# First norm of a hybrid decoder layer: root on ScalarE alone, whole-tile evictions on VectorE, another order of loads and signals

## The chip, the cores and the metric

One core of a Trainium2 chip runs the whole layer in one launch. The metric is the device time of one execution in microseconds (us), the median over runs. All data is float32.

## The reference, cut to what matters

One layer of a decoder trunk over 528 rows (16 learned meta tokens, then 512 tokens) of 1024 channels:

```
h = concat(meta_tokens, x)                       # 528 x 1024
n = h * rsqrt(mean(h*h, -1) + 1e-6) * norm1_g    # the first norm: what the change touches
u = n @ w_in                                     # 1024 x 6213 columns for three mixers and the gates
u_shift = u[:, :1280] + (previous row - u[:, :1280]) * rwkv_mu
y_a = RWKV-7 time mixing of u_shift   (6 heads of 64, chunks of 64 steps)
y_b = stick-breaking attention        (5 heads)
y_c = forgetting attention            (5 heads)
h = h + (sum_i sigmoid(G_i) * (y_i @ W_i)) @ w_out
h = h + MoE(rms_norm(h) * norm2_g)    # 16 experts, 2 of one group of 4 for each token
return h[16:]
```

## The kernel before

The kernel gives every engine one program, written out by hand, and orders them by counting semaphores. A helper `done` adds one to a semaphore and lets the same engine wait for it, so the instructions of ACT, DVE and POOL run strictly one after the other on their engine. No planner is at work. What one engine does next is the order of its block in the file.

**Loads (SP, L370 to L398).** SP asks for the meta rows, the four 128-row tiles of x (`h[:, t, :]`, 512 KB each), the norm's weights `g1` (1024 values that land as 128 x 8, one value at a time), three pieces of w_in (1 MB each, 256 columns, that is two chunks of 128), and then 21 small parameter transfers that all count on `params_in`. The fourth piece waits until the first has been used.

**First norm (L662 to L697 on ACT, L938 to L968 on DVE, L1384 to L1397 on PE).** For the meta rows, and then for each of the four tiles, ACT squares and sums a row (L675, L688; the sum comes out by a read of the accumulator, listed under the same line). DVE makes the mean and adds 1e-6 (L947, L959), ACT takes logarithm and exponential with factor -0.5 (L671, L672), DVE scales the rows (L949, L964), PE turns them by eight transposes into PSUM (L1387, L1395), and the eviction multiplies with `g1` and writes the turned rows `nT`. Of each tile DVE evicts chunks 0 to 3 in one instruction (L955) and ACT chunks 4 to 7 in four (L684). Ahead of tile 0's mean, DVE waits for `g1` (L950) in its program order. A constant `eps_c` (1e-6) is set on DVE after all of that (L968).

**Shifted columns (PE L1421 to L1447).** PE multiplies `nT` with ten chunks of 128 columns. One chunk has two halves of 264 rows, and 32 MATMUL records in the trace. Ahead of chunk n (from n = 2 on) it waits until chunk n-2 has been moved out of PSUM by ACT (L745), and ahead of both halves of chunk 0 it waits for the evictions of tiles 0 and 1, and 2 and 3. ACT's first eviction stands behind its wait for all 21 parameter transfers (L696, L697). DVE, behind the same wait, scales the router's weights (L970), clears padding (L975, L976) and mixes each chunk with its shifted copy (L982, L983). After chunk 1 is mixed ACT takes a tanh (L748) that the two low-rank products of chunks 2 to 4 need (L1400, L1406).

**Constants (POOL, L517 to L562).** POOL builds the masks one after another, with level masks for the later triangular inverses (L540 to L555), a row `reset` for the running sums, and some index rows. One signal at the end, `consts_ready`, counts 1 for all of them. DVE waits for it at L999, ahead of its first running sum (L987, which reads `reset`), PE at L1439 ahead of its first sum over heads (which reads `head_ones`). The level masks are first read by DVE at L1052.

After that PE works through projections for the attentions, the scan of the time mixing, both attentions, gate products, the output projection and the experts.

Of the kernel before, what the change touches and what calls it, by code (L numbers as in the profile page):

```python
# [14 lines left out]
ALU = mybir.AluOpType  # L15
# [3 lines left out]
P = 128  # L19
# [79 lines left out]
def hybrid_layer(nc, x, meta, g1, w_in, mu, w_up, w0, a_up, a0, k_k, k_a, r_k, ln_g, ln_b, f_b, q_g, k_g,  # L99
# [4 lines left out]
    with ExitStack() as ctx:  # L104
# [264 lines left out]
        def _(sp):  # L369
            sp.dma_start(metax[0:META, :], meta).then_inc(sem("meta_in"), 16)  # L370
            for t in range(NT):
                sp.dma_start(h[:, t, :], x[t * P:(t + 1) * P, :]).then_inc(sem(f"tile_in{t}"), 16)
            sp.dma_start(g1c, g1.rearrange("(c p) -> p c", p=P)).then_inc(sem("g1_in"), 16)
# [134 lines left out]
        def _(pool):  # L508
# [28 lines left out]

            for lv in range(6):
# [17 lines left out]
            done(g.memset(reset[:], 1.0))  # L556
            done(g.memset(reset[:, 0:L:CH], 0.0))
# [105 lines left out]
        def _(act):  # L663
# [6 lines left out]
            def inverse_root(z, s):  # L670
# [3 lines left out]
            act.wait_ge(sem("meta_in"), 16)  # L674
            done(a.activation(tmp_shift[0:META, :, :].rearrange("p a b -> p (a b)")[:, 0:D], metax[0:META, :], ACT.Square,  # L675
                              accum_out=stat[0:META, 4:5]), "ss_ready")
            act.wait_ge(sem("ms_ready"), 1)
            inverse_root(stat[0:META, 4:5], "rstd_ready")

            def high_chunks_out(t):  # L680
                act.wait_ge(sem("xT_psum"), t + 2)
                for c in range(T_SPLIT, DC):
                    o = 1024 * t + c * P
                    ins = a.activation(nT[:, c, META + t * P:META + (t + 1) * P], psf[:, o:o + P], ACT.Copy, scale=g1c[:, c:c + 1])  # L684
                done(ins, "nT_high")
# [253 lines left out]
        def _(dve):  # L939
# [3 lines left out]

            for j in range(SC):
                done(v.memset(U[:, j, 0:1], 0.0))
            dve.wait_ge(sem("ss_ready"), 1)
            done(ts(stat[0:META, 4:5], stat[0:META, 4:5], 1.0 / D, EPS, ALU.mult, ALU.add), "ms_ready")  # L947
            dve.wait_ge(sem("rstd_ready"), 1)
            done(ts(metax[0:META, :], metax[0:META, :], stat[0:META, 4:5], None, ALU.mult), "xs_ready")  # L949
            dve.wait_ge(sem("g1_in"), 16)  # L950
            gain = lambda c1, n: g1c[:, 0:c1].rearrange("p (c a) -> p c a", a=1).broadcast_to([P, c1, n])

            def low_chunks_out(t):
                dve.wait_ge(sem("xT_psum"), t + 2)
                done(tt(nT[:, 0:T_SPLIT, META + t * P:META + (t + 1) * P],  # L955
                        psf[:, 1024 * t:1024 * t + T_SPLIT * P].rearrange("p (c n) -> p c n", c=T_SPLIT), gain(T_SPLIT, P), ALU.mult), "nT_low")
# [985 lines left out]
```

## Time and profile before

| | us |
|---|---|
| median of 3 runs | 935.89 (935.33 to 936.1) |
| the profiled execution | 936.31 |
| its span in the trace | 934.6 |
| PE busy | 874.3 (94%) |
| DVE, ACT, POOL busy | 285.3, 196.8, 100.9 |
| mean granted TensorE clock | 0.974 of full |

PE is TensorE's matrix products, PEld its weight loads, DVE is VectorE, ACT is ScalarE, POOL is GpSimd, SPq the queue that issues transfers. Times in the rows are counted from the start of the span. "Releaser" is what ended an idle time. The granted clock is a share of 2.4 GHz, so 0.50 is 1.2 GHz. The profiled execution's time is 1.7 us more than its span, and 0.4 us more than the median.

### The profile page before, as it was taken

The page shows a single profiled execution, that of the slowest core. Times are in us where ns is not written, and L with a number is a line of the kernel's source. Part 1 is how long each engine was busy: PE and PEld are TensorE (multiplying, and loading weights), DVE is VectorE, ACT ScalarE, POOL GpSimd, SP SyncE. Part 2 cuts the span into 40 slices and gives each one's busy share as a digit, 9 for nine tenths or more (in the row PEclk, how much of TensorE's full clock was granted, in tenths as well). Part 3 has the DMA queues.
Part 4 walks back from the last instruction along what each step waited for, and adds up shares of the span by engine and source line. Part 5 has one row for each costly group of instructions (what it writes and reads, how often), then busy time and mean ns, then how long its engine had stood idle before and what let it go on. Part 6 is the DMA issues. An engine that isn't in the chain of part 4 may idle for free.

```text
span 934.6 us, 16279 instructions
## 1 busy us (share of the span) xinstructions
PE 874.3 (94%) x6948; PEld 505.8 (54%) x6948; DVE 285.3 (31%) x587; ACT 196.8 (21%) x390; POOL 100.9 (11%) x225
## 2 busy tenths in 40 slices
PE   3999999999998999999999999997999957999995
PEld 3878888877776765445454444443445542333331
DVE  3244811312312222452302244333531143222212
ACT  5135111122026111241412121143002220111100
POOL 7720000000003100011000000000000001212121
PEclk9999999999999999999999999998999967999998
DMA  8212136000000000047111112025565077899972
GB/s 228 58 46 88 47 80 193 2 2 3 2 3 1 3 3 25 23 101 199 46 50 32 50 54 68 1 76 177 168 230 227 22 282 281 290 380 386 384 274 110
DMA packets 76135, 109.76 MB, mean 117 GB/s; under 512 B 16891, under 2 KB 61067, under 8 KB 71968
## 3 DMA queue, kind: packets, MB, share of 16 engines
q1 hardware_dynamic: 71296, 93.22, 29.3%
q0 software_dynamic: 4768, 15.52, 5.7%
q8 instruction: 55, 0.90, 0.4%
q14 instruction: 16, 0.13, 0.0%
HBM read 100.32 MB, written 10.50 MB: 119 GB/s over the span
## 4 chain that ended last, share of the span: by engine, by line
PE 90%; DVE 3%; DMA 2%; ACT 2%; issue 1%; SPq 0%; DVEq 0%; POOL 0%; POOLq 0%; ACTq 0%
PE ps L1489 18%; PE ps L1514 10%; PE ps L1841 9%; PE ps L1466 8%; PE ps L1433 8%; PE ps L1793 6%; PE ps L1754 5%; PE ps L1867 5%; PE ps L1471 4%; PE ps L1828 1%; PE ps L1669 1%; PE ps L1737 1%; PE ps L1711 1%; DMA arena<-in_w_p_fox 1%; PE ps L1687 1%
## 5 line engine op out<-in xcount | busy, mean ns | idle before, releaser
L1489 PE MATMUL ps<-arena 128*128 128x512 f32 x304 | 142.9, 608 | 0.0
L1489 PEld LDWEIGHTS ps<-arena 128*128 128x128 f32 x304 | 54.8, 191 | 62.6 <-issue 60.7
L1841 PE MATMUL ps<-arena 128*32 128x512 f32 x624 | 86.0, 598 | 0.1
L1514 PEld LDWEIGHTS ps<-arena 64*64 64x64 f32 x2376 | 73.3, 134 | 23.7 <-issue 13.7
L1514 PE MATMUL ps<-arena 64*64 64x64 f32 x2376 | 80.3, 220 | 1.6 <-ACT arena L780 1.3
L1433 PE MATMUL ps<-arena 128*128 128x264 f32 x320 | 74.8, 393 | 0.6 <-PE ps L1433 0.6
L1433 PEld LDWEIGHTS ps<-arena 128*128 128x128 f32 x320 | 61.2, 193 | 13.5 <-issue 1.8
L1466 PE MATMUL ps<-arena,h 128*128 128x264 f32 x256 | 65.5, 397 | 0.5 <-PE ps L1433 0.5
L1754 PE MATMUL ps<-yT_all,arena 128*128 128x512 f32 x112 | 52.6, 623 | 5.3 <-DMA arena<-in_w_p_fox 5.1
L1793 PE MATMUL ps<-arena 128*128 128x512 f32 x128 | 56.2, 594 | 0.0
L1466 PEld LDWEIGHTS ps<-arena,h 128*128 128x128 f32 x256 | 45.9, 188 | 9.6 <-issue 0.8
L1841 PEld LDWEIGHTS ps<-arena 128*32 128x32 f32 x624 | 22.9, 109 | 45.1 <-issue 45.1
L1867 PE MATMUL ps<-arena 128*32 128x512 f32 x384 | 43.7, 594 | 0.6 <-DVE arena L1309 0.6
L1471 PE MATMUL ps<-arena 128*128 128x320 f32 (+1 forms) x128 | 42.7, 458 | 0.0
L1292 DVE TENSOR_TENSOR arena<-ps,chan 128x512 f32<-128x512 f32 x24 | 15.6, 686 | 83.4 <-PE ps L1828 83.3
L603 POOL DMA_INDIRECT arena<-n_rows,idx x12 | 11.8, 983 | 259.5 <-DVE idx L1276 252.7
L1754 PEld LDWEIGHTS ps<-yT_all,arena 128*128 128x128 f32 x112 | 21.6, 198 | 32.3 <-issue 25.4
L1793 PEld LDWEIGHTS ps<-arena 128*128 128x128 f32 x128 | 23.7, 189 | 28.2 <-issue 28.2
L1489 PE MATMUL ps<-arena,yT_all 128*128 128x512 f32 x80 | 38.1, 608 | 0.3 <-PE ps L1617 0.3
L1841 PE MATMUL ps<-yT_all,arena 128*32 128x512 f32 x144 | 36.4, 602 | 0.0
L780 ACT ACTIVATE arena<-ps 128x576 f32<-128x576 f32 x15 | 9.8, 652 | 81.7 <-PE ps L1514 81.7
L1042 DVE COPY arena<-ps 128x512 f32<-128x512 f32 x16 | 10.9, 680 | 50.0 <-PE ps L1489 50.0
(342 smaller groups left out, 1019.4 us busy)
## 6 DMA issues: line engine op xcount, KB each, us to landing
arena<-in_moe_w_down SPq DMA_DIRECT2D x32, 512.0 KB, 15.9
arena<-in_moe_w_gate SPq DMA_DIRECT2D x13, 1024.0 KB, 11.0
arena<-in_moe_w_up SPq DMA_DIRECT2D x13, 1024.0 KB, 16.3
arena<-in_w_in SPq DMA_DIRECT2D x19, 512.0 KB, 3.9
arena<-in_w_in SPq DMA_DIRECT2D x5, 1024.0 KB, 9.5
h<-in_x SPq DMA_DIRECT2D x8, 512.0 KB, 5.1
arena<-in_w_out SPq DMA_DIRECT2D x1, 4096.0 KB, 14.7
h<-in_w_in SPq DMA_DIRECT2D x3, 1024.0 KB, 5.1
```

The costliest lines, as they stand in the source:

```text
L603: g.indirect_dma_start(out=xg[s], out_offset=None, in_=n2_dram[:, :], in_offset=bass.IndirectOffsetOnAxis(ap=idx[:, col:col + 1], axis=0)) ...
L1042: done(v.tensor_copy(gate(n), ps[:, gate_bank(n), :]), "gate_out")
L1292: v.tensor_tensor(xgT[:, s, 4 * k:4 * k + 4, :], ps[:, k, :].rearrange("p (c n) -> p c n", c=4), g2p[:, 4 * k:4 * k + 4].rearrange("p (c a ...
L1433: ins = mm(ps[:, o + hf, 0:HALF], w[:, c, j * P:(j + 1) * P], nT[:, c, hf * HALF:(hf + 1) * HALF], start=(c == 0), stop=(c == DC - 1))
L1466: ins = mm(ps[:, b, 0:HALF], w[:, c, (j % 2) * P:(j % 2 + 1) * P], nT[:, c, k * HALF:(k + 1) * HALF], start=(c == 0), stop=(c == DC - 1))
L1471: ins = mm(ps[0:r, b, 0:nw], nT[:, c, k0:k0 + r], w[:, c, 0:nw], start=(c == 0), stop=(c == DC - 1))
L1489: ins = mm(ps[:, gate_bank(n), :], weights_of_gate(n)[:, c, :], nT[:, c, META:L], start=(c == 0), stop=(c == DC - 1))
L1514: ins = mm(psf[q, 512 * bank + c * CH:512 * bank + (c + 1) * CH], lhs(q, c), rhs(q, c), start=True, stop=True)
L1754: ins = mm(ps[:, bank(b), :], wpr[dc % 2][:, 3 * b + c, :], yT[b][:, c, :], start=(c == 0), stop=(b == 0 and c == 2), skip_group_check=(b ...
L1793: ins = mm(ps[:, out_bank(t, k), :], merged[:, c, t * P:(t + 1) * P], wout[:, c, k * 512:(k + 1) * 512], start=(c == 0), stop=(c == DC - 1))
L1841: ins = mm(ps[rs, bank, :].rearrange("p (h n) -> p h n", h=2), xgT[:, s, c, rs], w1[ws][:, :, c, :], start=(c == 0), stop=(c == DC - 1))
L1867: ins = mm(ps[rs, 4 + k, :], hT[:, s, c, rs], w2[ws][c][:, 512 * k:512 * k + 512], start=(c == 0), stop=(c == 1))
```

## The change

ACT now takes the whole root: Square with sum, then Ln with scale 1/1024 and bias `eps_c`, then Exp with factor -0.5 (`first_norm`). DVE's mean instructions go, and `eps_c` is set first on DVE. Tile 0 is handled ahead of the meta rows, in the loads and on ACT, DVE and PE. DVE evicts all eight chunks of tiles 0 to 2 in one instruction of 128 x 1024 each, and ACT only chunks 4 to 7 of tile 3. `g1` is asked for after tile 0 and the meta rows, ahead of tiles 1 to 3. POOL sets `reset` ahead of the level masks and signals twice: once after `reset`, once at the end. Waits on the full constants move to DVE ahead of L1044 and to PE ahead of L1508.

```diff
         def _(sp):
+            sp.dma_start(h[:, 0, :], x[0:P, :]).then_inc(sem("tile_in0"), 16)
             sp.dma_start(metax[0:META, :], meta).then_inc(sem("meta_in"), 16)
-            for t in range(NT):
+            sp.dma_start(g1c, g1.rearrange("(c p) -> p c", p=P)).then_inc(sem("g1_in"), 16)
+            for t in range(1, NT):
                 sp.dma_start(h[:, t, :], x[t * P:(t + 1) * P, :]).then_inc(sem(f"tile_in{t}"), 16)
-            sp.dma_start(g1c, g1.rearrange("(c p) -> p c", p=P)).then_inc(sem("g1_in"), 16)
...
+            done(g.memset(reset[:], 1.0))
+            done(g.memset(reset[:, 0:L:CH], 0.0), "consts_ready")
             for lv in range(6):
...
-            done(g.memset(reset[:], 1.0))
-            done(g.memset(reset[:, 0:L:CH], 0.0))
...
             act.wait_ge(sem("ms_ready"), 1)
-            inverse_root(stat[0:META, 4:5], "rstd_ready")
...
+            def first_norm(ss, dump, src, rows):
+                done(a.activation(dump, src, ACT.Square, accum_out=ss))
+                done(a.activation(ss, ss, ACT.Ln, scale=1.0 / D, bias=eps_c[0:rows]))
+                done(a.activation(ss, ss, ACT.Exp, scale=-0.5), "rstd_ready")
             for t in range(NT):
                 act.wait_ge(sem(f"tile_in{t}"), 16)
-                done(a.activation(xs[:, t, :], h[:, t, :], ACT.Square, accum_out=stat[:, t:t + 1]), "ss_ready")
-                act.wait_ge(sem("ms_ready"), t + 2)
-                inverse_root(stat[:, t:t + 1], "rstd_ready")
+                first_norm(stat[:, t:t + 1], xs[:, t, :], h[:, t, :], P)
                 if t == 0:
-                    act.wait_ge(sem("g1_in"), 16)
-                if t >= 1:
-                    high_chunks_out(t - 1)
-            high_chunks_out(NT - 1)
+                    act.wait_ge(sem("meta_in"), 16)
+                    first_norm(stat[0:META, 4:5], ..., metax[0:META, :], META)
+            act.wait_ge(sem("g1_in"), 16)
+            act.wait_ge(sem("xT_psum"), NT + 1)
+            ... (four evictions of tile 3, then "nT_high")
...
+            done(v.memset(eps_c, EPS), "ms_ready")
...
+            def chunks_out(t, c1):
+                dve.wait_ge(sem("xT_psum"), t + 1 if t == 0 else t + 2)
+                done(tt(nT[:, 0:c1, META + t * P:META + (t + 1) * P],
+                        psf[:, 1024 * t:1024 * t + c1 * P].rearrange("p (c n) -> p c n", c=c1), gain(c1, P), ALU.mult), "nT_low")
             for t in range(NT):
-                dve.wait_ge(sem("ss_ready"), t + 2)
-                done(ts(stat[:, t:t + 1], stat[:, t:t + 1], 1.0 / D, EPS, ALU.mult, ALU.add), "ms_ready")
+                dve.wait_ge(sem("rstd_ready"), t + 1 if t == 0 else t + 2)
+                done(ts(xs[:, t, :], h[:, t, :], stat[:, t:t + 1], None, ALU.mult), "xs_ready")
                 if t == 0:
-                    dve.wait_ge(sem("xT_psum"), 1)
+                    dve.wait_ge(sem("rstd_ready"), 2)
+                    done(ts(metax[0:META, :], metax[0:META, :], stat[0:META, 4:5], None, ALU.mult), "xs_ready")
+                    dve.wait_ge(sem("g1_in"), 16)
+                if t >= 1:
+                    chunks_out(t - 1, DC)
+                if t == 1:
+                    dve.wait_ge(sem("xT_psum"), 2)
                     done(tt(nT[:, :, 0:META], ps[:, 7, 0:DC * META]..., gain(DC, META), ALU.mult), "nT_meta")
-                dve.wait_ge(sem("rstd_ready"), t + 2)
-                done(ts(xs[:, t, :], h[:, t, :], stat[:, t:t + 1], None, ALU.mult), "xs_ready")
-                if t >= 1:
-                    low_chunks_out(t - 1)
-            low_chunks_out(NT - 1)
-            done(v.memset(eps_c, EPS))
+            chunks_out(NT - 1, T_SPLIT)
...
+            dve.wait_ge(sem("consts_ready"), 2)
             bc = lambda m_: m_.rearrange("p (a t) -> p a t", a=1).broadcast_to([P, NCH, CH])
...
-            pe.wait_ge(sem("xs_ready"), 1)
-            (meta transposes)
             for t in range(NT):
-                pe.wait_ge(sem("xs_ready"), t + 2)
+                pe.wait_ge(sem("xs_ready"), 1 if t == 0 else t + 2)
                 (eight transposes of tile t; ahead of tile 3 also a wait for nT_meta)
+                if t == 0:
+                    pe.wait_ge(sem("xs_ready"), 2)
+                    (meta transposes)
...
                             pe.wait_ge(sem("nT_low"), 2 * hf + 2)
-                            pe.wait_ge(sem("nT_high"), 2 * hf + 2)
+                            if hf == 1:
+                                pe.wait_ge(sem("nT_high"), 1)
...
             pe.wait_ge(sem("fill_out"), 2)
+            pe.wait_ge(sem("consts_ready"), 2)
```

## Rows read from the trace of the kernel before

**Rows 1.** The page: busy time of each engine.
```profile
PE 874.3 (94%) x6948; PEld 505.8 (54%) x6948; DVE 285.3 (31%) x587; ACT 196.8 (21%) x390; POOL 100.9 (11%) x225
```

**Rows 2.** The chain of waits to 160 us: start, length, what.
```profile
3.12 7.07 DMA chan<-in_norm_g
...
23.08 15.96 PE ps L1433 x64
...
39.33 7.37 PE ps L1433 x32
...
89.24 14.51 PE ps L1433 x64
```

**Rows 3.** Timeline of tile 1's root: start, length, engine, line, operation.
```profile
10.98 1.06 ACT L688 ACTIVATE arena<-h 128x1024 f32<-128x1024 f32 x1
...
12.23 0.15 DVE L959 TENSOR_SCALAR stat<-stat 128x1 f32<-128x1 f32 x1 [0.43 <-ACT arena L688]
12.48 0.20 ACT L671 ACTIVATE stat<-stat 128x1 f32<-128x1 f32 x1 [0.35 <-DVE stat L959]
...
12.72 0.20 ACT L672 ACTIVATE stat<-stat 128x1 f32<-128x1 f32 x1
...
13.03 0.75 DVE L964 TENSOR_SCALAR arena<-h,stat 128x1024 f32<-128x1024 f32 x1 [0.64 <-ACT stat L672]
```

**Rows 4.** Timeline: loads of x, the first Square, two evictions.
```profile
1.25 1.83 SPq L372 DMA_DIRECT2D h<-in_x  x4
...
5.19 1.06 ACT L688 ACTIVATE arena<-h 128x1024 f32<-128x1024 f32 x1 [0.35 <-DMA h<-in_x]
...
10.45 0.29 DVE L962 TENSOR_TENSOR arena<-ps,chan 128x128 f32<-128x128 f32 x1
...
13.94 0.69 DVE L955 TENSOR_TENSOR arena<-ps,chan 128x512 f32<-128x512 f32 x1 [0.16 <-PE ps L1395]
```

**Rows 5.** Transfers of x (all four, last line of the view).
```profile
DMA to landing us min/median/max: 3.9/5.5/7.2
```

**Rows 6.** PE's own timeline up to the dense products.
```profile
5.86 1.01 PE L1387 MATMUL ps<-ident,arena 16*128 16x16 f32 x8 [5.86 <-DVE arena L949]
11.86 3.94 PE L1395 MATMUL ps<-ident,arena 128*128 128x128 f32 x16 [5.00 <-DVE arena L964]
18.01 1.09 PE L1395 MATMUL ps<-ident,arena 128*128 128x128 f32 x8 [2.20 <-DVE arena L964]
21.11 1.97 PE L1395 MATMUL ps<-ident,arena 128*128 128x128 f32 x8 [2.01 <-DVE arena L964]
```

**Rows 7.** Stretches: length, PE, PEld, DVE, ACT, POOL busy (instructions), clock, DMA share, GB/s.
```profile
19.60:21.10 1.50, 0.00 (x0) 0.00 (x0) 0.83 (x3) 1.28 (x6) 1.28 (x4) 0.50 0.30 2
22.90:26.30 3.40, 3.40 (x9) 2.67 (x9) 0.75 (x2) 1.14 (x4) 2.74 (x11) 0.50 0.26 58
26.40:39.00 12.60, 12.60 (x57) 10.37 (x55) 4.04 (x8) 0.82 (x2) 10.03 (x40) 1.00 0.16 9
```

**Rows 8.** Timeline: what stands behind the last parameter transfer.
```profile
31.18 0.20 ACT L697 ACTIVATE chan<-chan 128x1 f32<-128x1 f32 x1 [6.86 <-DMA rw<-in_moe_we]
31.99 0.61 ACT L745 ACTIVATE arena<-ps 128x528 f32<-128x528 f32 x1 [0.61 <-PE ps L1433]
...
35.35 0.77 DVE L983 SCALAR_TENSOR_TENSOR arena<-arena,chan 128x528 f32<-128x528 f32 x1
...
41.43 1.28 ACT L748 ACT_TABLE_LOAD   x1 [1.70 <-DVE arena L983]
42.72 0.64 ACT L748 ACTIVATE arena<-arena 64x528 f32<-64x528 f32 x1
...
46.62 1.17 PE L1406 MATMUL ps<-arena,up_w 64*128 64x264 f32 x8
```

**Rows 9.** POOL's timeline at the end of its constants.
```profile
55.19 0.16 POOL L562 IOTA choice_id<- 128x8 f32 x1
```

**Rows 10.** DVE's first running sum, from the timeline.
```profile
57.51 1.26 DVE L987 TENSOR_TENSOR_SCAN arena<-reset,arena 128x528 f32<-128x528 f32 x1
```

More of the change, by code:

```diff
@@ L673, in _ @@
             log_exp_tables()
-            act.wait_ge(sem("meta_in"), 16)
-            done(a.activation(tmp_shift[0:META, :, :].rearrange("p a b -> p (a b)")[:, 0:D], metax[0:META, :], ACT.Square,
-                              accum_out=stat[0:META, 4:5]), "ss_ready")
             act.wait_ge(sem("ms_ready"), 1)
-            inverse_root(stat[0:META, 4:5], "rstd_ready")
[L680 to L685, printed above, removed]
+            def first_norm(ss, dump, src, rows):
+                done(a.activation(dump, src, ACT.Square, accum_out=ss))
+                done(a.activation(ss, ss, ACT.Ln, scale=1.0 / D, bias=eps_c[0:rows]))
+                done(a.activation(ss, ss, ACT.Exp, scale=-0.5), "rstd_ready")
             for t in range(NT):
                 act.wait_ge(sem(f"tile_in{t}"), 16)
-                done(a.activation(xs[:, t, :], h[:, t, :], ACT.Square, accum_out=stat[:, t:t + 1]), "ss_ready")
-                act.wait_ge(sem("ms_ready"), t + 2)
-                inverse_root(stat[:, t:t + 1], "rstd_ready")
+                first_norm(stat[:, t:t + 1], xs[:, t, :], h[:, t, :], P)
                 if t == 0:
-                    act.wait_ge(sem("g1_in"), 16)
-                if t >= 1:
-                    high_chunks_out(t - 1)
-            high_chunks_out(NT - 1)
+                    act.wait_ge(sem("meta_in"), 16)
+                    first_norm(stat[0:META, 4:5], tmp_shift[0:META, :, :].rearrange("p a b -> p (a b)")[:, 0:D], metax[0:META, :], META)
+            act.wait_ge(sem("g1_in"), 16)
+            act.wait_ge(sem("xT_psum"), NT + 1)
+            t = NT - 1
+            for c in range(T_SPLIT, DC):
+                o = 1024 * t + c * P
+                ins = a.activation(nT[:, c, META + t * P:META + (t + 1) * P], psf[:, o:o + P], ACT.Copy, scale=g1c[:, c:c + 1])
+            done(ins, "nT_high")
             act.wait_ge(sem("params_in"), 336)
@@ L942, in _ @@
             ts, tt, stt = v.tensor_scalar, v.tensor_tensor, v.scalar_tensor_tensor
+            done(v.memset(eps_c, EPS), "ms_ready")
             for j in range(SC):
                 done(v.memset(U[:, j, 0:1], 0.0))
[L946 to L949, printed above, removed]
@@ L950, in _ @@
-            dve.wait_ge(sem("g1_in"), 16)
             gain = lambda c1, n: g1c[:, 0:c1].rearrange("p (c a) -> p c a", a=1).broadcast_to([P, c1, n])
[L953 to L956, printed above, removed]
+            def chunks_out(t, c1):
+                dve.wait_ge(sem("xT_psum"), t + 1 if t == 0 else t + 2)
+                done(tt(nT[:, 0:c1, META + t * P:META + (t + 1) * P],
+                        psf[:, 1024 * t:1024 * t + c1 * P].rearrange("p (c n) -> p c n", c=c1), gain(c1, P), ALU.mult), "nT_low")
@@ L1144, in _ @@
             steps = DC * (gates_out - EARLY_GATES)
-            dve.wait_ge(sem("consts_ready"), NT + 1)
+            dve.wait_ge(sem("consts_ready"), NT + 2)
             def biased(u):
@@ L1384, in _ @@
             pe.wait_ge(sem("ident_ready"), 1)
-            pe.wait_ge(sem("xs_ready"), 1)
-            for c in range(DC):
-                ins = tr(ps[:, 7, c * META:(c + 1) * META], metax[0:META, c * P:(c + 1) * P], ident[0:META, 0:META])
-            ins.then_inc(sem("xT_psum"), 1)
             for t in range(NT):
-                pe.wait_ge(sem("xs_ready"), t + 2)
+                pe.wait_ge(sem("xs_ready"), 1 if t == 0 else t + 2)
                 if t == NT - 1:
@@ L1396, in _ @@
                 ins.then_inc(sem("xT_psum"), 1)
+                if t == 0:
+                    pe.wait_ge(sem("xs_ready"), 2)
+                    for c in range(DC):
+                        ins = tr(ps[:, 7, c * META:(c + 1) * META], metax[0:META, c * P:(c + 1) * P], ident[0:META, 0:META])
+                    ins.then_inc(sem("xT_psum"), 1)
             pe.wait_ge(sem("nT_meta"), 1)
```

## The prediction

> **What bounds the kernel now.** The busy shares come first: PE is busy 94% of the span [rows 1], so only time in which PE stands still, or runs at a lower clock, can be won. The chain of waits, read next, shows where that is near the change. Until 23.08 us the chain runs over loads, ACT, DVE and short groups of transposes, and its largest piece is 7.07 us of waiting for the norm's weights. From 23.08 on it is PE on L1433, without a break but for 0.29 us [rows 2]. The dense products start only when tile 3's transposes are through, so the end of the first norm sets the start of a stretch that is bound by PE. A microsecond won ahead of 23.08 is a microsecond of the whole, unless something with a fixed time of its own then becomes late. PE's own timeline says how empty that time is: idle of 5.86, 5.00, 2.20 and 2.01 us between four groups [rows 6]. The stretches say at which clock: it was granted 0.50, that is 1.2 GHz, after PE's idle time, still 0.50 over 22.9 to 26.3 with PE fully busy, and 1.00 (2.4 GHz) from 26.4 on [rows 7].
>
> **Part 1: loads and root.** Tile 0 takes the meta rows' place in the queue. Four issues take 1.83, so 0.46 each, and its own comes at 0.79 in place of 1.25 [rows 4]. Before, ACT could start on it at 5.19 [rows 4], 3.9 us after its issue [rows 5]. I take 4.7 (bounds: 4.5, with the meta rows' 64 KB no longer ahead of it, and 5.2 as before). DVE's instruction falls out of the root. Before, Square began at 10.98, the mean at 12.23, Ln at 12.48, Exp at 12.72, the scaling at 13.03 [rows 3]. Now Ln can begin at about Square + 1.20, Exp at + 1.44, the scaling at + 1.75, and ACT's next Square at + 1.68 (0.24 after Exp, as Exp is after Ln). That is 0.3 us less for each tile, and since ACT no longer evicts tiles 0 to 2 (four instructions, 1.14 us a tile), it runs ahead of everyone. Squares begin at 4.7 (tile 0), 6.4 (meta), 8.0, 9.7 and 11.4 (tiles 1 to 3).
>
> Are tiles 1 to 3 there in time? They were issued at 1.7, 2.2 and 2.6 and the slowest took 7.2 us [rows 5]; if that was the last, tile 3 landed at about 9.8. Now the 1024 single values of `g1` are in front. Their price is not shown apart; from below it is nothing (they were in the same stream before), from above, since the chain had `g1` landing at 3.12 + 7.07 = 10.19 [rows 2], 0.4 us after that tile and amid other data, I allow 1.4 us. Tile 3 is then there by 9.8 to 11.2, against 11.4. I take it as hidden. `g1` itself, issued at about 1.7, would land by 8.8 even if it took the 7.07 us again, and DVE wants it at 10.6.
>
> The Trainium skill speaks against this edit: DMA: Bandwidth & Descriptors (Bandwidth, table of measured sizes, and the rules for kernel authors) says that transfers under 64 KB are mostly overhead, and gives 0.68 us of engine time for 4 KB. By that figure, an estimate, tile 3 would land 0.7 us later, at 10.5, still ahead of ACT; no row here shows the transfer by itself.
>
> **Part 2: DVE and PE to the last transpose.** DVE scales a tile in 0.75 us [rows 3], and I take the same for the 16 meta rows of the same length. The eviction of 128 x 1024 doesn't occur before. From 128 x 128 in 0.29 and 128 x 512 in 0.69 [rows 4] each further 128 columns cost 0.134 us, so 1.23 us; bounds are 0.69 and twice that, 1.38. With 0.04 us between instructions of one engine (12.68 to 12.72) and up to 0.1 between engines (12.92 to 13.03, [rows 3]): tile 0 scaled 6.45 to 7.20; PE turns it 7.26 to 9.24 (the first two tiles took 3.94, as slow as the last at half clock, [rows 6]); meta scaled 8.1 to 8.9, turned 9.2 to 10.2 (1.01); tile 1 scaled 9.8 to 10.54, turned 10.6 to 12.6; tile 0 evicted 10.58 to 11.81; meta evicted to 12.14; tile 2 scaled 12.2 to 12.9, turned from 13.0; tile 1 evicted 13.0 to 14.2; tile 3 scaled 14.2 to 15.0. PE begins on tile 3 at 15.03, where it began at 21.11, and needs 1.09 us at the full clock or 1.97 at half [rows 6]. The dense products begin at 16.1 or 17.0, against 23.08: 7.0 or 6.1 us earlier. DVE sets this, no longer ACT: its six instructions from 9.8 to 15.0 stand in a row. With the eviction's bounds the two in this row move it by -1.1 to +0.3 us.
>
> Chunk 0's first half wants tiles 0 and 1, evicted at 14.2; its second half wants tile 3, whose last four chunks ACT writes 1.14 us after the transposes, while the first half takes at least 3.6 us (a quarter of 14.51, [rows 2]). Neither waits.
>
> **Part 3: the clock.** PE now is nearly without a gap from 7.26 on: idle 0.4, 0.4 and 0.1 us if the clock is at half. Before, the half clock followed on gaps of 2 us, and cost 15.96 - 14.51 = 1.45 us of the first two chunks [rows 2] besides 0.88 of the transposes. I expect the full clock to be granted before 14, and transposes then finish sooner, so gaps of about 1 us come back; it may drop again. The ends: no clock gain, dense from 17.0, chunk 1 through at 33.0; full gain, dense from 16.1, chunk 1 through at 30.6.
>
> The Trainium skill's page TensorE: Matmul & The Clock Gate (What's actually happening) says "the default state is throttled, and activity releases the throttle". By that rule the full gain is due, and the dense products start at 2.4 GHz. This trace agrees as to direction: 0.50 while idle, 1.00 after PE had been busy [rows 7].
>
> **Part 4: what is late next.** The 21 parameter transfers don't move: their issue is behind the same 5 MB of loads (four tiles, three pieces), and the last landed at 31.1 [rows 8]. ACT's first eviction stands behind them. In the kernel before this cost nothing, since chunk 0 was done only at 31.9 [rows 8]. Now chunk 0 is done at 23.4 to 25.7, ACT multiplies at 31.18, evicts at 31.4 to 32.04, and chunk 2 can't start before 32.1. It started at 39.33 [rows 2], so no more than 7.2 us can be won there. A second limit is close behind: DVE is bound by the same wait and ended its mixing of chunk 0 at 36.12 [rows 8]; chunk 1 takes 1.5 more, 37.65; then table load 1.28 and tanh 0.64 after 0.08, so 39.7. The low-rank product wants that tanh; it started at 46.62 to 46.69, after chunk 2. With chunk 2 from 32.1 to 39.45 it starts at 39.75: 6.9 us won. With no clock gain chunk 2 starts at 33.25 and the product at 40.6: 6.1 won. One slow stretch of 3.4 us after 16 costs 1.7 and still fits under the cap (30.6 + 1.7 + 0.3 = 32.6, 6.7 won).
>
> **Part 5: constants.** `reset` now comes ahead of the level masks; POOL's work is the same, and its end stays at 55.35 [rows 9]. DVE's running sum wants only `reset`. It began at 57.51 [rows 10] and would begin at 50.6 now; chunk 3's mixing, which is behind the same wait, 1.5 earlier at 49. Held to 55.35 it would be where it was. The new waits for the second signal stand behind all ten shifted chunks, past 103 us (89.24 + 14.51, [rows 2]), and cost nothing with the masks done at 55.35. The memset of `eps_c` moved to the front is 0.06 us under the table load. `nT_high` and the fewer waits are nothing.
>
> **Sum.** 6.9 us less from the first low-rank product on, behind which PE is bound by its own work. The profiled execution took 936.31, which gives 929.4; it stood 0.42 over the median of the runs, so 929.0.
>
> **Rivals.**
> A. The clock stays at half, or falls again and again, up to the dense products: 6.1 us won, 929.8. For it: 0.50 was held for over 3 us of full load [rows 7]. Against it: the denser PE.
> B. The last parameters land later than 31.1, or tiles do: some of the 6.9 goes. Each microsecond is one of the total. Tile 3 at 13 in place of 11.4 costs next to nothing at PE, since DVE takes it at 14.2. Parameters at 33 cost 1.9, 930.9. For it: `g1` needed 7.07 us to land, so a small transfer in a full queue is slow. Against: the same bytes are ahead of them.
> C. The parameter cap doesn't bite, because less is queued when SP comes to them: up to 7.2 to 8.4 us won (7.0 + 1.45), 927.5 to 928.7.
> D. The change doesn't do what it says: POOL's masks still hold DVE, at 55.35. Then chunk 3's sums are where they were and nothing is won, 935.9. Against: the first signal is behind `reset` alone.
> E. The other side. The order of loads pushes the parameters back. ACT and DVE stand in order behind the wait, PE behind ACT's eviction, so every microsecond past 31.1 goes into the whole from the start. It gives back the 6.9 when they land at 38, and is 2 us slower than before from 40 on, 938. Nothing in the rows speaks for 7 us.
>
> **How the numbers follow.** The sum's case 0.60, A 0.17, B 0.11, C 0.08, D 0.02, E 0.02. The predicted time is the first's. About 0.2% (1.9 us) is what a measurement of this kernel can tell from no change. B reaches 931 with most of its chance; the clock's later drops and the eviction's bounds add 0.5 each way. I give 927.7 to 931.0. Faster by more than 0.2%: the sum, A, C and nearly all of B, 0.95. Same: D and a rest, 0.03. Slower: E, 0.02.
>
> **What would show it.** PE's transposes of tile 3 at about 15.0 and L1433 from 16.1 to 17.0; ACT idle up to 31.2 with the last parameters as releaser, and L745 twice in a row right after; PE idle of about 1 us ahead of chunk 2 with ACT L745 as releaser, if the clock was full; L1406 at 39.8; L959 gone; L987 not behind 55.35; all later lines shifted by one amount. Wrong it would be if DVE's 1024-wide evictions took over 1.4 us, if ACT waited on x's tiles, if parameters landed elsewhere than 31, or if later stages did not keep the shift.

## The result, and the profile after

The changed kernel takes 930.39 us (median; 928.7 to 932.88), the kernel before on the same chip 935.77. The ratio is 0.9943, with a 95% interval of 0.9932 to 0.9955: 5.4 us less, where 6.9 were forecast. The profiled execution took 929.94, with a span of 928.2, which is 6.4 under the span before. Three stray executions (1040.72 and 3052.37 us of the kernel before, 1776.19 of e6 below) are not in any ratio. One profile's last microseconds have to be read with care: the eight executions of the changed kernel lie up to 4.2 us apart, and what this comes with is shown below.

PE's busy time fell by 2.3 us. The shifted columns' line now has idle ahead of it, put down to ACT's eviction. The page's busy line and one of its groups (the line moved from L1433 to L1431; columns: busy us and mean ns of one, then idle before and its releaser). Of other lines that appear below, L1489 is L1487 now, and L1754 is L1753.

```profile
PE 872.0 (94%) x6948; PEld 504.3 (54%) x6948; DVE 286.4 (31%) x582; ACT 193.8 (21%) x378; POOL 103.2 (11%) x225
...
L1431 PE MATMUL ps<-arena 128*128 128x264 f32 x320 | 73.0, 386 | 1.8 <-ACT arena L743 1.5
```

The timeline of the changed kernel to the dense products (start, length, engine, line, operation, idle before and who ended it):

```profile
5.66 1.06 ACT L678 ACTIVATE arena<-h 128x1024 f32<-128x1024 f32 x1 [3.60 <-DMA h<-in_x]
...
6.84 0.29 ACT L679 ACTIVATE stat<-stat,chan 128x1 f32<-128x1 f32 x1
...
7.17 0.20 ACT L680 ACTIVATE stat<-stat 128x1 f32<-128x1 f32 x1
...
7.49 0.75 DVE L953 TENSOR_SCALAR arena<-h,stat 128x1024 f32<-128x1024 f32 x1 [5.32 <-ACT stat L680]
...
8.39 1.94 PE L1387 MATMUL ps<-ident,arena 128*128 128x128 f32 x8 [8.39 <-DVE arena L953]
...
10.93 0.54 POOL L539 MEMSET reset<- 128x528 f32 x1
10.99 1.03 DVE L953 TENSOR_SCALAR arena<-h,stat 128x1024 f32<-128x1024 f32 x1 [1.03 <-ACT stat L680]
...
12.06 1.22 DVE L949 TENSOR_TENSOR arena<-ps,chan 128x1024 f32<-128x1024 f32 x1
...
14.45 3.14 PE L1387 MATMUL ps<-ident,arena 128*128 128x128 f32 x16 [0.41 <-DVE arena L953]
...
17.43 14.42 PE L1431 MATMUL ps<-arena 128*128 128x264 f32 x64
```

PE's idle times of 5.00, 2.20 and 2.01 us [rows 6] are gone; 0.79 and 0.41 are left. Its first tile starts at 8.39 in place of 11.86, the dense products at 17.4 in place of 22.9 to 23.08 [rows 2], and their first two chunks take 14.4 in place of 15.96. Chunk 1 therefore ends 7.2 us earlier (31.85 against 39.04). What follows there is in the same timeline:

```profile
29.25 0.58 SPq L399 DMA_DIRECT2D rw<-in_moe_we  x1
...
32.38 0.20 ACT L695 ACTIVATE chan<-chan 128x1 f32<-128x1 f32 x1 [13.52 <-DMA rw<-in_moe_we]
...
32.61 1.26 ACT L743 ACTIVATE arena<-ps 128x528 f32<-128x528 f32 x2
...
33.37 7.37 PE L1431 MATMUL ps<-arena 128*128 128x264 f32 x32 [1.52 <-ACT arena L743]
34.25 1.52 DVE L971 MEMSET arena<- 128x1755 f32 x1 [0.43 <-ACT arena L743]
...
38.95 1.28 ACT L746 ACT_TABLE_LOAD   x1 [5.08 <-DVE arena L978]
```

ACT waits 13.5 us for the last parameters, then evicts two chunks in a row. PE has stood still for 1.52 us by then. The last parameters were expected by 31.2 [rows 8] and came 1.2 later. SP's own timeline shows where that arose; first before, then after:

```profile
24.86 1.21 SPq L398 DMA_DIRECT2D chan<-in_norm_g  x2
...
28.02 0.58 SPq L398 DMA_DIRECT2D rw<-in_moe_we  x1
```

```profile
25.23 2.08 SPq L399 DMA_DIRECT2D chan<-in_norm_g  x2
...
29.25 0.58 SPq L399 DMA_DIRECT2D rw<-in_moe_we  x1
```

SP issues one transfer after the other. It came to this pair 0.37 us later than before, and one of the two issues took 1.45 in place of about 0.6. So the last issue is 1.23 late, and from it to ACT's multiply it is 3.1 to 3.2 us in both kernels. The bytes ahead of the parameters were the same: the time went in the issues, not in the transfer. The chain of waits of the changed kernel runs over SP's issues to the last transfer, and through DVE's clearing and mixing and ACT's table load and tanh it comes to the low-rank product:

```profile
29.25 3.05 DMA rw<-in_moe_we
...
40.94 1.17 PE ps L1403 x8
...
83.52 14.51 PE ps L1431 x64
```

The first low-rank product starts at 40.9 (before: 46.62 [rows 8]), 5.7 us earlier, and chunks 8 and 9 at 83.52 against 89.24 [rows 2], again 5.7. That number is what the change's own stretch brought in these two profiles. The other 0.7 of the 6.4 in the span came later, at stretches of half clock. The chains of both kernels show it; first before, then after (start, length, what):

```profile
428.45 5.35 PE ps L1489 x12
...
501.08 6.93 PE ps L1489 x12
...
642.65 8.71 PE ps L1754 x14
```

```profile
422.36 7.05 PE ps L1487 x12
...
496.97 5.35 PE ps L1487 x12
...
636.94 8.26 PE ps L1753 x14
```

Equal work of 12 records takes 5.35 at full clock and up to 7.05 where the clock fell. The kernel before paid at 501 us and the changed one at 422, which cancels: the shift is 5.7 again behind both. At 641 (634) both have a stretch of half clock of 6.83 us. It lay over 0.9 us more of the piece at 643 (637) in the kernel before, which cost that one 0.45, and a longer one, from 757 (750) on, another 0.2.

A stretch of 3.41 us costs up to 1.7 us and comes at other places or not at all in other executions. In the traces of all fourteen kernels here, the time from the low-rank product to the end goes with it. It is 885.6 and 885.8 us in e11 and e5, which have no such stretch between 45 and 630 us; 887.3 to 887.5 with one at 422 to 425 (the changed kernel, e3, e6); 888.0 to 888.6 with one at 494 to 501 (before, e7, e8, e9, e12); and 889.7 to 890.5 with two, or with one of 6.83 us (e10, e4, e2). e1 has none and 886.9. These 5 us lie behind all that the change touches, and the executions of the changed kernel differ by 4.2.

One thing the record does not hold: it has no granted clock for the first 14 to 23 us, and a view of the profile prints 1.00 there. Where the text below says half pace in that time, it is read from the length of eight transposes of a tile. They took 1.97 where 0.50 was granted (21.1 to 22.9 in the kernel before) and 1.09 where 1.00 was (18.0 to 19.1).

### The profile page after: what moved, and what is told of

Same layout as the page of the kernel before. It is cut to its first block, busy times and chain, and to the rows that moved or that the text cites. A ratio compares the mean times of both kernels' runs of the same rounds, so it can differ in the third digit from the quotient of the medians.

```text
span 928.2 us, 16250 instructions
## 1 busy us (share of the span) xinstructions
PE 872.0 (94%) x6948; PEld 504.3 (54%) x6948; DVE 286.4 (31%) x582; ACT 193.8 (21%) x378; POOL 103.2 (11%) x225
## 4 chain that ended last, share of the span: by engine, by line
PE 88%; SPq 3%; DVE 3%; DMA 2%; issue 1%; ACT 1%; DVEq 0%; POOL 0%; POOLq 0%; ACTq 0%
PE ps L1487 19%; PE ps L1513 10%; PE ps L1840 9%; PE ps L1464 8%; PE ps L1792 6%; PE ps L1431 5%; PE ps L1753 5%; PE ps L1866 5%; PE ps L1469 4%; SPq L399 2%; PE ps L1827 1%; PE ps L1668 1%; PE ps L1736 1%; PE ps L1710 1%; DMA arena<-in_w_p_fox 1%
## 5 line engine op out<-in xcount | busy, mean ns | idle before, releaser
L1487 PE MATMUL ps<-arena 128*128 128x512 f32 x304 | 143.0, 608 | 0.0
L1487 PEld LDWEIGHTS ps<-arena 128*128 128x128 f32 x304 | 54.8, 191 | 62.7 <-issue 60.8
L1431 PE MATMUL ps<-arena 128*128 128x264 f32 x320 | 73.0, 386 | 1.8 <-ACT arena L743 1.5
L1431 PEld LDWEIGHTS ps<-arena 128*128 128x128 f32 x320 | 59.9, 189 | 14.1 <-issue 3.3
L1753 PE MATMUL ps<-yT_all,arena 128*128 128x512 f32 x112 | 52.2, 619 | 5.2 <-DMA arena<-in_w_p_fox 5.1
L1840 PEld LDWEIGHTS ps<-arena 128*32 128x32 f32 x624 | 22.9, 109 | 44.9 <-issue 44.9
L1288 DVE TENSOR_TENSOR arena<-ps,chan 128x512 f32<-128x512 f32 x24 | 15.6, 687 | 83.1 <-PE ps L1827 83.0
L1792 PEld LDWEIGHTS ps<-arena 128*128 128x128 f32 x128 | 23.7, 189 | 28.2 <-issue 28.2
L1753 PEld LDWEIGHTS ps<-yT_all,arena 128*128 128x128 f32 x112 | 21.4, 197 | 32.0 <-issue 25.1
L1487 PE MATMUL ps<-arena,yT_all 128*128 128x512 f32 x80 | 38.1, 608 | 0.3 <-PE ps L1616 0.3
L1469 PEld LDWEIGHTS ps<-arena 128*128 128x128 f32 x128 | 21.9, 189 | 7.6
```

Of the source, the lines that this page charges most:

```text
L1288: v.tensor_tensor(xgT[:, s, 4 * k:4 * k + 4, :], ps[:, k, :].rearrange("p (c n) -> p c n", c=4), g2p[:, 4 * k:4 * k + 4].rearrange("p (c a ...
L1431: ins = mm(ps[:, o + hf, 0:HALF], w[:, c, j * P:(j + 1) * P], nT[:, c, hf * HALF:(hf + 1) * HALF], start=(c == 0), stop=(c == DC - 1))
L1469: ins = mm(ps[0:r, b, 0:nw], nT[:, c, k0:k0 + r], w[:, c, 0:nw], start=(c == 0), stop=(c == DC - 1))
L1487: ins = mm(ps[:, gate_bank(n), :], weights_of_gate(n)[:, c, :], nT[:, c, META:L], start=(c == 0), stop=(c == DC - 1))
L1753: ins = mm(ps[:, bank(b), :], wpr[dc % 2][:, 3 * b + c, :], yT[b][:, c, :], start=(c == 0), stop=(b == 0 and c == 2), skip_group_check=(b ...
L1792: ins = mm(ps[:, out_bank(t, k), :], merged[:, c, t * P:(t + 1) * P], wout[:, c, k * 512:(k + 1) * 512], start=(c == 0), stop=(c == DC - 1))
```

## The experiments

The second column is the start of the first low-rank product in the profile, read from PE's timeline. It is the best measure of the stretch, as later clock stretches are not in it, but it stands for one execution each; those of e2 (936.19), e10 (934.44) and e4 (932.98) were 5.3, 5.1 and 3.1 us over their medians. Before: 46.6. The changed kernel: 40.9. e1 to e4, e5 to e8 and e9 to e12 ran on three chips, each beside the kernel before, whose medians were 934.88, 935.20 and 934.94. The changed kernel stood only beside the first four. Across the groups the ratios are what to compare.

| kernel | product at | median us | ratio to before (95%) |
|---|---|---|---|
| e1 the change again | 40.75 | 929.42 | 0.9940 (0.9923 to 0.9958) |
| e2 + 8 transfers | 43.92 | 930.87 | 0.9947 (0.9933 to 0.9962) |
| e3 parameter wait moved | 41.15 | 929.38 | 0.9935 (0.9921 to 0.9948) |
| e4 one signal | 41.04 | 929.86 | 0.9935 (0.9920 to 0.9950) |
| e5 norm weights last | 40.80 | 930.26 | 0.9950 (0.9930 to 0.9969) |
| e6 before, norm weights early | 42.84 | 932.36 | 0.9969 (0.9957 to 0.9982) |
| e7 ACT evicts too | 43.52 | 933.42 | 0.9976 (0.9964 to 0.9988) |
| e8 before, root on ACT | 45.41 | 934.41 | 0.9989 (0.9978 to 1.0000) |
| e9 before, PE kept busy | 43.84 | 933.27 | 0.9965 (0.9950 to 0.9980) |
| e10 change, PE kept busy | 43.04 | 929.34 | 0.9947 (0.9926 to 0.9967) |
| e11 = e10 + e3 | 40.31 | 928.07 | 0.9919 (0.9904 to 0.9934) |
| e12 parameters first | 39.40 | 930.07 | 0.9941 (0.9921 to 0.9961) |

**e1, the change again.**

> The changed kernel itself, on the same chip as the next three, so that they have something to stand against. If the last parameter landed at 32.3 us in the profiled execution only by chance (one transfer, the second of the norm's weights, was held 1.45 us in its queue), it lands near 31.5 here and the first low-rank product starts near 40.1; if the new order of loads causes it, it lands at 32.3 again and the product starts at 40.9. Time about 929.9.

Parameters landed at 32.15, not at 31.5, though the second transfer of the norm's weights was not held: in e1 it was another issue, of `a_up`, that held SP (1.64 in place of 0.60). With loads moved forward and nothing added to the parameters, ACT or DVE got past that wait at 32.15 to 33.06 in all six profiles that show it (the change, e1, e4, e5, e7, e10), and at 32.7 in e6; with the old order at 31.18 (before), 31.14 (e8), but 32.25 in e9. One issue held by about 1 us is found in the change, in e1 to e6 and in e9 to e11, at six different transfers, and in neither before nor e8, the two that were early. In e7 no issue was held, and from the last issue to ACT it was 4.1 us in place of e1's 3.2. So the old order can be late too, and the order of loads is part of it at most. What holds an issue stays open.

**e2, later parameters.**

```diff
             par = sem("params_in")
+            spare = sb("spare", [P, 8])
+            for k_ in range(8):
+                sp.dma_start(spare[:, k_:k_ + 1], mu.rearrange("(c p) -> p c", p=P)[:, k_:k_ + 1]).then_inc(par, 16)
...
-            act.wait_ge(sem("params_in"), 336)
+            act.wait_ge(sem("params_in"), 336 + 128)
...
-            dve.wait_ge(sem("params_in"), 336)
+            dve.wait_ge(sem("params_in"), 336 + 128)
```

> The changed kernel with eight more small transfers (128 values each into a tile that nothing reads) ahead of the 21 parameter transfers, counted on the same semaphore. Theory (the wait for the parameters is the bound from 31 us on): each costs 0.49 us of issue, so parameters land 3.9 us later, the low-rank product starts 3.9 later, and the whole is 3.9 slower than the changed kernel, 933.8. Rival (the wait is only shown last, PE's own work is the bound): the first 1 to 2 us are free, the whole is 2 to 2.9 slower. Rival (queues absorb it): nothing.

The eight delayed the landing by only 1.8 us, because part of their issue fell where the queue was held anyway: in e1 the first two parameters took 2.93 and 3.64 to issue, in e2 all eight took 6.29 and the two behind them 0.43 and 1.84. But what they did delay went through one for one: ACT's multiply at 33.95 in place of 32.15 (e1), chunk 2 at 34.95 in place of 33.14. PE's own timeline of e2:

```profile
17.72 15.04 PE L1434 MATMUL ps<-arena 128*128 128x264 f32 x64
34.95 9.05 PE L1434 MATMUL ps<-arena 128*128 128x264 f32 x32 [2.19 <-ACT arena L746]
43.92 1.17 PE L1406 MATMUL ps<-arena,up_w 64*128 64x264 f32 x8
```

PE waited although its dense work began 0.9 later and ran slower at first, so the parameters are the bound. The 9.05 in place of 7.37 is new: after PE's idle time the clock fell (granted 0.53 over 35.9 to 38.0). In this execution the wait for the parameters was paid twice. The median is only 1.45 over e1's, the intervals of the two overlap, and neither the forecast's 3.9 nor the rival's 2 to 2.9 was met.

**e3, the parameter wait moved.**

```diff
-            act.wait_ge(sem("params_in"), 336)
-            done(a.mul(qg8, qgc, 0.125))
...
                 if n == 1:
+                    act.wait_ge(sem("params_in"), 336)
+                    done(a.mul(qg8, qgc, 0.125))
...
-            dve.wait_ge(sem("params_in"), 336)
-            done(tt(rw[:], rw[:], g2c..., ALU.mult))
             for t_ in (At, Rt, Bt, Kt):
                 done(v.memset(t_[:, :, L:LP], 0.0))
             done(v.memset(Pc[:], 1.0))
+            dve.wait_ge(sem("params_in"), 336)
...
             for n in range(3):
                 mixed(n, *(["wd_mixed"] if n == 1 else []))
+            done(tt(rw[:], rw[:], g2c..., ALU.mult))
```

> The changed kernel with the wait for the parameters moved: ACT evicts chunks 0 and 1 first, DVE clears its padding (2.9 us) first and scales the router's weights after the third mixing. Theory: chunk 2 starts at once after chunk 1 (32.15 in place of 33.37), mixing starts at 32.4 in place of 35.8 and the tanh is done by 37.5, so the low-rank product starts at 39.5 in place of 40.94: 1.4 us faster than the changed kernel, 928.5. Rival (something else is late just behind, as DVE's or ACT's order in the later chunks): nothing or less than 0.5.

The median didn't move. PE's timeline of e3 shows what stood in the way in one execution:

```profile
14.31 4.02 PE L1387 MATMUL ps<-ident,arena 128*128 128x128 f32 x16 [0.40 <-DVE arena L953]
18.12 15.43 PE L1431 MATMUL ps<-arena 128*128 128x264 f32 x64
33.85 7.37 PE L1431 MATMUL ps<-arena 128*128 128x264 f32 x32 [0.30 <-PE ps L1431]
```

The wait on ACT is gone; only the 0.30 of issue is left, as before. But in this execution the last transposes (4.02 for two tiles, 3.14 in the changed kernel's profile) and the start of the dense products ran at half pace, and chunk 1 ended at 33.55, when the wait on ACT would have been nearly over anyway (33.1 to 33.4 in e1 and the changed kernel). Clock and parameters are two limits of nearly the same height here. That fits the rival "something else is late just behind", with the clock as that something. It is read from one profile and not shown for the other five executions; e10 to e12 try it.

**e4, one signal.** `reset` is set at the end of POOL's constants again, one signal, the waits as before.

> The changed kernel with the constants signalled once, at their end, as before; all else of the change is kept. Theory: DVE's mixing of chunk 3 and its running sum are held to 55.4 as they were before, so DVE falls 5 to 6 us behind, and the sums over heads that PE wants after chunk 5 come as late as before: most of the 5.8 us is given back, 934 to 935.5. Rival (DVE has slack in the shifted chunks): the delay is made up before PE wants anything of DVE, 930.

DVE was held as forecast, but PE did not notice. First two rows of e4's timeline, then its list of PE's waits between 30 and 160 us (total, times, longest), in which DVE does not stand:

```profile
55.30 0.71 DVE L977 TENSOR_TENSOR arena<-arena 128x528 f32<-128x528 f32 x1 [12.05 <-POOL choice_id L563]
...
66.23 1.94 PE L1413 MATMUL ps<-arena,head_ones 128*128 128x264 f32 x8
```

```profile
PE ps L1430 <- ACT arena L743: 2.0, 1, 2.0
...
PE ps L1402 <- ACT arena L746: 0.3, 1, 0.3
```

The mixing of chunk 3 came 5 us later than it could, and the first sums over heads were still reached by PE in its own time, at 66.2. In the changed kernel DVE stood idle for 4.3 to 7.1 us ahead of chunks 3, 4 and 5; in e4 it had made up the delay by chunk 5, ahead of which it waits for ACT again (3.71). The rival holds. The two-part signal is worth nothing by itself that these runs can tell.

**e5, the norm's weights last.** The line that asks for `g1` goes behind tiles 1 to 3.

> The changed kernel with the norm's weights asked for last again, behind tiles 1 to 3; tile 0 stays first. Theory: DVE waits for them at 10.2, where the changed kernel has it scale tile 1 from 11.0 on, so nothing is lost: 0 to 0.3 us slower, while the tiles land sooner. Rival (it was the 7.07 us wait that the change removed): 2 us or more slower.

The dense products began at 18.1 in place of e1's 16.86 (0.9 of it is tile 3 at half pace), but the low-rank product came at 40.80, as in e1, since chunk 2 waited for the parameters all the same (0.59). 0.8 us more in the median lies within both intervals. Once tile 0 goes first, the weights' place matters little as long as the parameters bound. The interval is too wide to call it nothing.

**e6, the norm's weights early, alone.**

```diff
             sp.dma_start(metax[0:META, :], meta).then_inc(sem("meta_in"), 16)
-            for t in range(NT):
+            sp.dma_start(h[:, 0, :], x[0:P, :]).then_inc(sem("tile_in0"), 16)
+            sp.dma_start(g1c, g1.rearrange("(c p) -> p c", p=P)).then_inc(sem("g1_in"), 16)
+            for t in range(1, NT):
                 sp.dma_start(h[:, t, :], ...)
-            sp.dma_start(g1c, g1.rearrange("(c p) -> p c", p=P)).then_inc(sem("g1_in"), 16)
```

> The kernel before with one part of the change alone: the norm's weights are asked for after the meta rows and tile 0. Theory: DVE waits no longer than tile 0's Square needs (6.9 us or so), so tile 0 starts 3.3 us earlier, and the loop of ACT, DVE and PE follows: 3.3 us less at the first dense product, more if the clock holds: 931 to 932.6. Rival (the wait was hidden): 935.8.

The low-rank product came 3.8 us earlier and the median fell by 2.8. PE's timeline: tile 0 at 8.11 (11.86 before), then steps of 3.2 to 3.4 us a tile, each at half pace.

```profile
8.11 1.97 PE L1396 MATMUL ps<-ident,arena 128*128 128x128 f32 x8 [1.24 <-DVE arena L965]
...
17.88 1.97 PE L1396 MATMUL ps<-ident,arena 128*128 128x128 f32 x8 [1.38 <-DVE arena L965]
19.64 15.60 PE L1434 MATMUL ps<-arena 128*128 128x264 f32 x64
35.55 7.37 PE L1434 MATMUL ps<-arena 128*128 128x264 f32 x32 [0.30 <-PE ps L1434]
```

This single move of one transfer brings about half of the whole gain (0.31% of 0.57%).

**e7, ACT evicts again.** Everything of the change, but ACT evicts chunks 4 to 7 of each tile and DVE 128 x 512.

> The changed kernel with ACT evicting chunks 4 to 7 of every tile as before, so VectorE's evictions are 128 x 512 again. Theory (parameters are the bound by now): the start of the dense products moves by up to 1 us (ACT's 1.14 us a tile come into its own row, DVE's 0.54 go out of its), later by 1 to 2 at worst, 18.5 in place of 17.4, and as PE then stood still for 1.5 us at chunk 2, most of it is free: 0 to 0.8 us slower than the changed kernel. Rival (whole-tile eviction is what brought the gain): 2 us or more slower.

The forecast of 0 to 0.8 us missed. The ratio is 0.9976 against e1's 0.9940, 3.4 us more, and the two intervals do not touch. Its ACT timeline has the four evictions between the Squares (10.98 to 12.13, then the next Square at 12.16), so ACT's row is 2.9 to 3.3 us a tile, and ACT sets the pace again:

```profile
18.04 1.97 PE L1391 MATMUL ps<-ident,arena 128*128 128x128 f32 x8 [1.28 <-DVE arena L957]
19.80 16.11 PE L1434 MATMUL ps<-arena 128*128 128x264 f32 x64
36.22 7.37 PE L1434 MATMUL ps<-arena 128*128 128x264 f32 x32 [0.30 <-PE ps L1434]
```

Dense products at 19.8 and half pace in them: 2.8 us of product start, past all slack that the parameter wait gave. With the evictions split, more than half of the gain is lost; with the weights' move alone (e6) about half is there. So these two parts make up about all of it, within the noise.

**e8, the root alone.** In the kernel before, DVE's mean instructions go and ACT takes Ln with scale and bias.

> The kernel before with ACT taking the whole root, everything else as it was. The wait for the norm's weights then stands ahead of DVE's scaling of tile 0 all the same. Theory: 0.35 us a tile on the three tiles behind it, and ACT starts on tile 1 early: 0.7 to 1.5 us less, 934.3 to 935.1. Rival (DVE's hop was hidden): nothing.

1.2 us at the low-rank product (45.41), 0.8 in the median, about 1 us in the ratio (upper end 1.0000): as forecast, at the edge of what can be told.

**e9, PE kept busy in the kernel before.**

```diff
                 ins.then_inc(sem("xT_psum"), 1)
+                if t in (1, 2):
+                    for _ in range(12):
+                        tr(ps[:, 6, 0:P], ident[:], ident[:])
```

> The kernel before with 12 idle transposes (of the identity, into a PSUM bank that tile 3 later overwrites) after tile 1 and again after tile 2, in PE's two idle times of 2.2 and 2.0 us. Theory (the half clock at the dense products comes from those idle times): the clock stays at full, the last transposes take 1.09 in place of 1.97 and the first two chunks 14.5 in place of 15.96; 2.3 us less than the kernel before where it ran them at half clock, 933.2 to 934. Rival (the idle work comes late or does not keep the clock): 935 or up to 1 us slower.

The idle work does the same to the clock as the change: 14.42 for the first two chunks, the last transposes in 1.09, and a granted clock of 1.00 over 17.8 to 36.0, where the kernel before had 0.50 from 19.6 to 26.3 [rows 7].

```profile
17.77 1.09 PE L1395 MATMUL ps<-ident,arena 128*128 128x128 f32 x8 [0.27 <-DVE arena L964]
18.70 1.47 PE L1399 MATMUL ps<-ident 128*128 128x128 f32 x12
20.88 1.09 PE L1395 MATMUL ps<-ident,arena 128*128 128x128 f32 x8 [0.71 <-DVE arena L964]
21.81 14.42 PE L1436 MATMUL ps<-arena 128*128 128x264 f32 x64
```

1.7 us less in the median, 2.8 at the low-rank product (0.2 of it is tile 0, which came earlier in this execution), without a single useful instruction moved. The half clock before the dense products came from the idle times.

**e10, PE kept busy in the changed kernel.** 22 idle transposes ahead of tile 0; 2, 5 and 4 before tiles 1, 2 and 3.

> The changed kernel with 22 idle transposes ahead of tile 0 and 2, 5 and 4 in the short gaps before tiles 1, 2 and 3. Theory (the first eviction, behind the parameters, is the bound): the clock is full from about 8 us on, the dense products run at full clock whatever the run, and chunk 2 still starts at 33.1 to 33.4: no gain in the best runs (928), slow ones of 930 to 932 are fewer, median 0 to 1 us less than the changed kernel. Rival (the clock is the bound in most runs): 1.5 to 2.5 us less.

Dense products at 16.84 and at full clock, and nothing of it arrives: the median is e1's. Against the expectation, the clock was not full from 8 us on: tile 0's transposes at 7.95 still took 1.97, though PE had turned idle work from 1.41 to 6.37. The first full clock in the record is at 14.0. The stretches of e10 (length, PE, PEld, DVE, ACT, POOL busy, granted clock, DMA share, GB/s), behind PE's line at chunk 2:

```profile
34.05 9.05 PE L1437 MATMUL ps<-arena 128*128 128x264 f32 x32 [2.80 <-ACT arena L743]
```

```profile
31.30:34.00 2.70, 0.00 (x0) 0.00 (x0) 0.68 (x3) 0.87 (x3) 2.15 (x9) 1.00 0.97 165
...
34.50:37.80 3.30, 3.30 (x10) 2.48 (x9) 2.80 (x3) 0.05 (x1) 2.77 (x9) 0.50 0.44 152
```

PE was ready at 31.3, waited 2.80 for the parameters (33.06 here), and the clock was 0.50 right after. The faster start was turned into idle time, and that into a slower chunk 2. This is one of the slow executions of e10 (934.44); four of its seven lie between 928.8 and 929.3, and whether the clock fell in those is not on record.

**e11, both limits taken away.** e3 and e10 together.

> The idle transposes and the moved wait for the parameters together. Theory (two limits of nearly the same height, clock and parameters, each of which hides the other): chunk 2 starts at 31.6 to 31.8, the low-rank product at 39.1, 1.6 to 1.8 us ahead of the changed kernel, 927.3 to 928, where the moved wait alone brought nothing. Rival (a third limit stands at the same height): 929.4 as before.

928.07, the best median of all, 1.35 under e1. In its profile the third tile still ran at half pace (18.30 for the dense start, later than forecast), the clock then held, and PE has no wait left in the shifted columns. The product started at 40.31, not at 39.1: the forecast's time held to 0.1 us, but not its path. The intervals of e1 and e11 overlap, so that it beats the changed kernel is likely, not shown; that it beats the kernel before by more than 6 us (0.9919) is.

**e12, parameters behind the first piece.**

> The changed kernel with the 21 parameter transfers issued behind the first 1 MB piece, ahead of the second and third. Theory: they land by 24 to 27 us, the wait no longer bounds, chunk 2 starts right after chunk 1 (31.6 at full clock, 33.3 at half), the second piece lands at 28 to 30 and is just in time: 0 to 1.6 us less than the changed kernel, as the clock falls. Rival (the second piece is now late): chunk 2 waits for a transfer, 1 to 3 us slower.

Parameters at 28.01 (a microsecond past the forecast's 24 to 27), chunk 2 right after chunk 1, at 32.10, the product at 39.40: the cap is gone and 1.35 us are won against e1 at this place. So the parameters alone can be the bound when the clock is full by then. PE's timeline of e12:

```profile
17.38 14.42 PE L1432 MATMUL ps<-arena 128*128 128x264 f32 x64
32.10 7.37 PE L1432 MATMUL ps<-arena 128*128 128x264 f32 x32 [0.30 <-PE ps L1432]
```

The median (930.07, from 927.63 to 933.65) does not show it; six executions that scatter by 6 us can't resolve 1.3. In the profile the win was given back at 494 us, where the half clock came for 3.41.

## Why the prediction was right, and by how much it was not

**Bound and direction: right.** Time won ahead of the dense products was time of the whole until the parameter wait. The measured time lies in the range, 1.4 us over the forecast. From the first low-rank product to 360 us every product of PE is 5.7 us earlier, as "all later lines shifted by one amount" said.

**Part 1, loads: tile 0 mis-sized, the rest right.** Square on tile 0 began at 5.66, outside the bounds of 4.5 to 5.2. Tile 0 as the first transfer of all landed 4.8 us after its issue, where it took 3.9 behind the meta rows [rows 5]. In the ten profiles with tile 0 first, Square begins between 5.09 (e2) and 5.76 (e7), and in the four with the meta rows first between 5.16 and 5.49. So handing tile 0 the first place brought no earlier Square at all; why is open. Ln took 0.29 in place of 0.20 [rows 3], so Square to scaling is 1.83 against 1.75. Tiles 1 to 3 were never waited for, as said. The estimate for the small transfer from the Trainium skill, DMA: Bandwidth & Descriptors (Bandwidth), made no difference that a run showed: ACT waited for none of tiles 1 to 3 in the changed kernel, nor in e5, where that transfer comes behind them.

**Part 2, DVE's row: right in form, 1.4 late.** The eviction took 1.22 to 1.23 (forecast 1.23). Tile 3 was reached at 16.5 in place of 15.03: 1.0 from tile 0 and 0.3 from one scaling that took 1.03 beside POOL's memset. Dense start 17.4 against 16.1 to 17.0, later than both ends. That cost nothing, as the parameters bounded behind it: luck, as far as this part goes. e7 shows that these evictions are worth 2.8 us at the low-rank product, half pace included.

**Part 3, the clock: right in kind, late in time.** The first two chunks took 14.4. The full clock came not before 14 but at 16.3, just ahead of tile 3. It differs by execution: e1, e4 and e12 have it at 15.6 to 16.1, e2, e3 and e5 at 18.4 to 20.2, and these turned tile 3 at half pace. e9 shows the mechanism by itself. The rule quoted from the Trainium skill, TensorE: Matmul & The Clock Gate (What's actually happening), holds in e9, where added activity kept the clock at 1.00; e10 shows its other side, a fall after one wait of 2.80 us.

**Part 4, the cap: the right mechanism, the size off by 1.2. This is the term that failed.** "The 21 parameter transfers don't move" was the step: they landed at 32.3 in place of 31.1, and chunk 2 started at 33.37, not 32.1; the low-rank product at 40.9, not 39.75. With it 5.7 us were won and not 6.9. The reason given, the same 5 MB ahead of them, is a sum of bytes, while their time is set by SP's issues: 0.37 us of the delay had built up ahead of the held pair, 0.86 is in it. e2's profile shows one microsecond at chunk 2 for each that they are late, e3 and e12 that the wait goes when it is moved or they are. That is rival B in small (given 0.11): the forecast's case and B are one mechanism with two sizes.

**Part 5, the constants: wrong in its price.** It was said that with one signal DVE would be held and, in rival D, that nothing would then be won. DVE is held (e4), PE isn't, and the time is 929.86 and not 935.9. The place of a wait was costed, not who waits for the engine behind it.

**The sum.** 6.9 were forecast; 6.4 in the profiled span, of which 5.7 in the stretch and 0.7 by clock stretches elsewhere; 5.4 in the medians. Rival A's half clock is there in part in the profiles of e2, e3 and e5; in e5 it cost nothing at the low-rank product, since the cap hid it. That the span came within 0.5 of the sum is luck to the extent of the 0.7.

## What to carry to other kernels

When a start is pulled forward, list every wait that ends at a fixed time of its own and stands behind it, with its scatter; the nearest one takes the rest of the gain, and here two stood at nearly the same height (parameters and clock), so that removing either alone brought nothing that the medians show. Count the issues of a queue, not only its bytes. Look for the one transfer that blocks an engine in program order: moving it by three places was about half the gain. Before paying for a finer signal, ask who waits for the engine that it frees, not only whether that engine waits.

## What the runs showed of the hardware that was not expected

Idle work on PE changes the time: 24 transposes of the identity made the kernel before 1.7 us faster (e9), through the granted clock. A wait of 2.2 to 2.8 us in dense work was followed by the half clock in e2 and e10 (chunk 2 in 9.05), one each of 1.5, 1.9 and 2.0 was not (7.37, the changed kernel, e1 and e4). A DVE scaling of 128 x 1024 took 1.03 in place of 0.75 where POOL set memory at the same time (the changed kernel, e3, e7), and in e1, where the scaling began first, it was POOL's memset that took 1.06 in place of 0.54 instead.
